# Negated scores with the sink as one more column, and the attention items of part 0 spread over all ten blocks of a group

## What is computed

```python
s = jnp.einsum('bnqkgd,bnskd->bnkgqs', q, k) * (HEAD_DIM ** -0.5)
s = s - slopes[...] * dist[...]
s = jnp.where(allowed[...], s, MASK_VALUE)
m = jnp.maximum(jnp.max(s, axis=-1), sink)
p = jnp.exp(s - m[..., None])
denom = jnp.sum(p, axis=-1) + jnp.exp(sink - m)
o = jnp.einsum('bnkgqs,bnskd->bnqkgd', p / denom[..., None], v)
y = (o * jax.nn.silu(gate)) @ w_out
```

## The kernel before

| slot | step | engine and line |
|---|---|---|
| 1 | S: scores into ps_s | PE L1003, L1004 |
| 1 | SM: scale, bias, row maximum; then neg_max, sink_arg | DVE L1351, L1358, L1359 |
| 1 | EX: four exponentials with row sum, sink_exp | ACT L1627, L1628 |
| 2 | SR: denom, recip; rows times recip | DVE L1367, L1368; GpSimd L1762 |
| 3 | TR: transposes into ps_t | PE L1022 |
| 3 | PH, PLO: high and low half, pt_hi and pt_lo | ACT L1636, DVE L1374 |
| 4 | PV: product with v into ps_o | PE L1049 |
| 4 | OG: half copy (sq<-ps_o), sum, times the gate | ACT L1645, DVE L1381, L1395 |
| 4 | YH, YL: the two halves of the result | ACT L1653, GpSimd L1741 |

## Time and profile before

### The profile page before, as it was taken

The page is one execution under the profiler, slowest core; times in us unless marked ns, Lnnn a source line. Parts: engine busy times, 40 slices in busy tenths (PEclk is TensorE's granted clock), DMA queues, the critical chain, the costliest instruction groups (busy, mean ns, idle before and its releaser), DMA issues.

```text
span 1758.8 us, 28031 instructions
## 1 busy us (share of the span) xinstructions
PE 1610.3 (92%) x9083; PEld 1373.4 (78%) x9083; DVE 869.8 (49%) x2194; ACT 746.0 (42%) x1658; POOL 417.4 (24%) x403
## 2 busy tenths in 40 slices
PE   5899699888788899999999899999998899999998
PEld 3788588878788777878887677878887687878877
DVE  3544423666663344337763345247662453257761
ACT  4333232666653422226664322246653422256552
POOL 0332143443443100112332000213232000213332
PEclk8889888999988999999999999999999999999998
DMA  8677767443443545543333555543325444543313
GB/s 299 227 268 245 247 233 248 145 145 133 156 143 105 211 168 191 196 164 128 136 120 144 180 191 189 184 151 135 120 97 191 167 174 165 192 171 121 136 59 143
DMA packets 145206, 299.86 MB, mean 170 GB/s; under 512 B 20719, under 2 KB 71231, under 8 KB 145070
## 3 DMA queue, kind: packets, MB, share of 16 engines
q1 hardware_dynamic: 145070, 298.08, 47.4%
HBM read 232.44 MB, written 65.79 MB: 170 GB/s over the span
## 4 chain that ended last, share of the span: by engine, by line
PE 71%; DVE 10%; issue 7%; ACT 7%; DMA 3%; POOL 1%; SPq 0%; DVEq 0%; ACTq 0%; POOLq 0%
PE ps_u L811 56%; PE ps_o L1049 4%; PE ps_t L1022 3%; PE ps_s L1003 2%; PE ps_s L1004 2%; ACT ps_u L1518 1%; DVE work L1351 1%; DVE ps_u L1195 1%; ACT work L1627 1%; POOL w_lo L1689 1%; DMA x_in<-in_ada_w_dram 1%; DVE work L1261 1%; DVE q_st L1235 1%; ACT silu_g L1535 1%; DVE ps_o L1381 1%
## 5 line engine op out<-in xcount | busy, mean ns | idle before, releaser
L811 PE MATMUL ps_u<-h_all_hi,w_hi 128*128 128x512 f32 (+2 forms) x1440 | 528.8, 367 | 32.2 <-DVE silu_g L1228 11.2
L811 PE MATMUL ps_u<-h_all_hi,w_lo 128*128 128x512 f32 (+2 forms) x1440 | 517.4, 359 | 0.0
L811 PE MATMUL ps_u<-h_all_lo,w_hi 128*128 128x512 f32 (+2 forms) x1440 | 517.4, 359 | 0.0
L811 PEld LDWEIGHTS ps_u<-h_all_hi,w_hi 128*128 128x128 f32 x1440 | 281.7, 196 | 82.4 <-issue 17.6
L811 PEld LDWEIGHTS ps_u<-h_all_hi,w_lo 128*128 128x128 f32 x1440 | 281.2, 195 | 36.9
L811 PEld LDWEIGHTS ps_u<-h_all_lo,w_hi 128*128 128x128 f32 x1440 | 281.6, 196 | 35.9 <-issue 1.4
L811 PE MATMUL ps_u<-y_hi,w_hi 128*128 128x512 f32 (+1 forms) x640 | 231.1, 361 | 7.1 <-POOL y_lo L1741 7.0
L811 PE MATMUL ps_u<-y_lo,w_hi 128*128 128x512 f32 (+1 forms) x640 | 228.4, 357 | 0.0
L811 PE MATMUL ps_u<-y_hi,w_lo 128*128 128x512 f32 (+1 forms) x640 | 228.3, 357 | 0.0
L1762 POOL TENSOR_TENSOR work<-work,recip 128x512 f32<-128x512 f32 (+2 forms) x136 | 132.8, 996 | 323.4 <-DVE recip L1368 323.4
L1689 POOL TENSOR_TENSOR w_lo<-w_raw,w_hi 128x1024 fp32r<-128x1024 f32 (+1 forms) x56 | 129.3, 2310 | 238.9 <-ACT w_hi L1431 207.2
(11 more groups left out here) (186 smaller groups left out, 2252.4 us busy)
## 6 DMA issues: line engine op xcount, KB each, us to landing
w_hi<-w_hi_kept SPq DMA_DIRECT2D x156, 512.0 KB, 3.5
w_lo<-w_lo_kept SPq DMA_DIRECT2D x156, 512.0 KB, 4.5
w_hi_kept<-w_hi SPq DMA_DIRECT2D x52, 512.0 KB, 5.1
w_lo_kept<-w_lo SPq DMA_DIRECT2D x52, 512.0 KB, 5.9
...
```

Source lines behind the costliest of these rows:

```text
L811: last = nc.tensor.matmul(out, w, x, start=(i == 0), stop=(i == n - 1))
```

## The change

The scale of the scores becomes negative, so row *minima* of the negated scores are taken; the scan starts from neg_sink (a value per row) instead of a constant and delivers neg_max at once. In front of the exponentials ACT writes neg_sink as one more column of each block, and the exponentials run over 257 columns with scale -1, so that their row sum is already the denominator. neg_max as an instruction of its own, sink_arg, sink_exp and denom disappear. The blocks of work are 260 columns apart.

Within a slot the order becomes S, PV, E1, SR, **SM, OG, EX**, E2, TR, PH, W, YH, PLO, YL, in all parts. In part 0, `places` puts a0 in q1-1, a1 in g0-1, a2 in g1-1, a3 in the next kv-0, a4 in q0-0 and a5 in q1-0 (the last group keeps its former places).

```diff
@@ slot @@
             out += [("PV", c)] if c is not None else []
-            out += first + to_norm + second
+            out += first + to_norm
+            out += [("SM", a)] if a is not None else []
             out += [("OG", c)] if c is not None else []
+            out += [("EX", a)] if a is not None else []
+            out += second
             out += [("TR", b), ("PH", b)] if b is not None else []
-            out += [("SM", a)] if a is not None else []
             out += [("split",)]
             out += [("YH", c)] if c is not None else []
-            out += [("EX", a)] if a is not None else []
             out += [("PLO", b)] if b is not None else []
@@ part @@
-            places = {("q1", 1): 0, ("g0", 1): 1, ("g1", 0): 2, ("g1", 1): 3, ("kv", 1): 4, ("q0", 0): 5}
+            places = {("q1", 1): 0, ("g0", 1): 1, ("g1", 1): 2, ("kv", 0): 3, ("q0", 0): 4, ("q1", 0): 5}
+            places_last = {("q1", 0): 5, ("q1", 1): 0, ("g0", 1): 1, ("g1", 0): 2, ("g1", 1): 3}
@@ SM on DVE @@
-                        last = V.tensor_tensor_reduce(out=out, in0=src, in1=b, scale=HEAD_DIM ** -0.5, scalar=LOWEST, op0=ALU.add,
-                                                      op1=ALU.max, accum_out=row_max[r, d, at:at + 1])
-                    link(last)
...
-                    link(V.scalar_tensor_tensor(out=m2(neg_max), in0=m2(row_max), scalar=-1.0, in1=ns, op0=ALU.mult, op1=ALU.min))
-                    V.tensor_tensor(m2(sink_arg), m2(neg_max), ns, ALU.subtract).then_inc(max_ready, 1)
+                        last = V.tensor_tensor_reduce(out=out, in0=src, in1=b, scale=-HEAD_DIM ** -0.5, scalar=neg_sink[r, h:h + 1],
+                                                      op0=ALU.add, op1=ALU.min, accum_out=neg_max[r, d, at:at + 1])
+                    last.then_inc(max_ready, 1)
@@ SR on DVE @@
-                    dve.wait_ge(sink_ready, a + 1)
-                    link(V.tensor_tensor(denom[r, d, 0:nb], row_sum[r, d, 0:nb], sink_exp[r, d, 0:nb], ALU.add))
-                    V.reciprocal(recip[r, d, 0:nb], denom[r, d, 0:nb]).then_inc(recip_ready, 1)
+                    dve.wait_ge(exp_ready, a + 1)
+                    V.reciprocal(recip[r, d, 0:nb], row_sum[r, d, 0:nb]).then_inc(recip_ready, 1)
@@ EX on ACT @@
+                    if a >= 2:
+                        act.wait_ge(p_turned, a - 1)
+                    put = work[r, d, 0:nb * BLOCK].rearrange("p (t e c) -> p t e c", e=2, c=BLOCK)[:, :, :, end]
+                    A(put, neg_sink[r, h0:h0 + 2].unsqueeze(1).to_broadcast([r.stop - r.start, nb // 2, 2]), ACT.Copy).then_inc(sink_put, 1)
+                    act.wait_ge(sink_put, a + 1)
...
-                        A(x, x, ACT.Exp, bias=neg_max[r, d, at:at + 1], accum_out=row_sum[r, d, at:at + 1])
-                    A(sink_exp[r, d, 0:nb], sink_arg[r, d, 0:nb], ACT.Exp).then_inc(sink_ready, 1)
+                        last = A(x, x, ACT.Exp, bias=neg_max[r, d, at:at + 1], scale=-1.0, accum_out=row_sum[r, d, at:at + 1])
+                    last.then_inc(exp_ready, 1)
```

More of the change, by code:

```diff
@@ L46 @@
 SHIFT = 2
-LOWEST = -3e38
+BLOCK = 260
 U_PROMPT = 2 * HIST
@@ L396, in part @@
                 for b, evacs in enumerate(blocks):
-                    at = places.get((what, b))
-                    a = src[at] if at is not None and src else None
+                    at = (places_last if p == 0 and g == GROUPS - 1 and what in ("q1", "g0", "g1") else places).get((what, b))
+                    from_old = p == 0 and (what, b) == ("q1", 0)
+                    its = old if from_old else src
+                    a = its[at] if at is not None and its else None
                     last = b == (1 if p == 0 else 0)
@@ L407, in part @@
                             s.append(x)
-        tail = [new[at] for (what, b), at in places.items() if what in ("kv", "q0")]
+        tail = new[4:] if p == 0 else new[3:]
         drain = [[x for x in slot(a) if x != ("split",)] for a in tail + [None, None, None]]
@@ L453, in trunk_kernel @@
         x_in = sb("x_in", [P, 2, D_MODEL])
-        work = sb("work", [P, 2, 4 * 256])
+        work = sb("work", [P, 2, 4 * BLOCK])
         pt_hi, pt_lo = sb("pt_hi", [P, 1024], F32R), sb("pt_lo", [P, 1024], F32R)
@@ L483, in trunk_kernel @@
         sinks, neg_sink = sb("sinks", [P, HEADS]), sb("neg_sink", [P, HEADS])
-        row_max, neg_max = sb("row_max", [P, 2, 4]), sb("neg_max", [P, 2, 4])
-        row_sum, sink_arg, sink_exp = sb("row_sum", [P, 2, 4]), sb("sink_arg", [P, 2, 4]), sb("sink_exp", [P, 2, 4])
-        denom, recip = sb("denom", [P, 2, 4]), sb("recip", [P, 2, 4])
+        neg_max, row_sum, recip = sb("neg_max", [P, 2, 4]), sb("row_sum", [P, 2, 4]), sb("recip", [P, 2, 4])
         flat = work[:, :, :].rearrange("p a b -> p (a b)")
@@ L1021, in _ @@
                                 o = (4 * (at // 2) + 2 * kt + e) * P
-                                last = nc.tensor.transpose(t_flat[:, o:o + P], work[:, a % 2, at * 256 + kt * P:at * 256 + (kt + 1) * P],
+                                last = nc.tensor.transpose(t_flat[:, o:o + P], work[:, a % 2, at * BLOCK + kt * P:at * BLOCK + (kt + 1) * P],
                                                            ident[:, :])
@@ L1345, in _ @@
                         if it["sample"]:
-                            out, src = work[r, d, at * 256:at * 256 + WINDOW + SAMPLE], s_flat[r, at * 256:at * 256 + WINDOW + SAMPLE]
+                            out, src = work[r, d, at * BLOCK:at * BLOCK + WINDOW + SAMPLE], s_flat[r, at * 256:at * 256 + WINDOW + SAMPLE]
                             b = bias[r, 2 * hp + e, 2 * WINDOW - WINDOW - SAMPLE:2 * WINDOW]
                         else:
-                            out, src = work[:, d, at * 256 + k0:at * 256 + 256], s_flat[:, at * 256 + k0:at * 256 + 256]
+                            out, src = work[:, d, at * BLOCK + k0:at * BLOCK + 256], s_flat[:, at * 256 + k0:at * 256 + 256]
                             b = bias[:, 2 * hp + e, k0:256]
-                        last = V.tensor_tensor_reduce(out=out, in0=src, in1=b, scale=HEAD_DIM ** -0.5, scalar=LOWEST, op0=ALU.add,
-                                                      op1=ALU.max, accum_out=row_max[r, d, at:at + 1])
-                    link(last)
-                    h0 = 4 * g + 2 * hp
-                    nt = nb // 2
-                    m2 = lambda x: x[r, d, 0:nb].rearrange("p (t e) -> p t e", e=2)
-                    ns = neg_sink[r, h0:h0 + 2].unsqueeze(1).to_broadcast([r.stop - r.start, nt, 2])
-                    link(V.scalar_tensor_tensor(out=m2(neg_max), in0=m2(row_max), scalar=-1.0, in1=ns, op0=ALU.mult, op1=ALU.min))
-                    V.tensor_tensor(m2(sink_arg), m2(neg_max), ns, ALU.subtract).then_inc(max_ready, 1)
+                        h = 4 * g + 2 * hp + e
+                        last = V.tensor_tensor_reduce(out=out, in0=src, in1=b, scale=-HEAD_DIM ** -0.5, scalar=neg_sink[r, h:h + 1],
+                                                      op0=ALU.add, op1=ALU.min, accum_out=neg_max[r, d, at:at + 1])
+                    last.then_inc(max_ready, 1)
                 elif kind == "SR":
@@ L1621, in _ @@
                     nb = 2 * len(it["tiles"])
+                    end = WINDOW + SAMPLE if it["sample"] else 256
+                    h0 = 4 * it["g"] + 2 * it["hp"]
+                    if a >= 2:
[3 more added lines that the diff above has]
+                    act.wait_ge(sink_put, a + 1)
                     act.wait_ge(max_ready, a + 1)
@@ L1625, in _ @@
                     for at, t, e, k0 in item_blocks(it):
-                        x = work[r, d, at * 256 + k0:at * 256 + (WINDOW + SAMPLE if it["sample"] else 256)]
-                        A(x, x, ACT.Exp, bias=neg_max[r, d, at:at + 1], accum_out=row_sum[r, d, at:at + 1])
-                    A(sink_exp[r, d, 0:nb], sink_arg[r, d, 0:nb], ACT.Exp).then_inc(sink_ready, 1)
+                        x = work[r, d, at * BLOCK + k0:at * BLOCK + end + 1]
+                        last = A(x, x, ACT.Exp, bias=neg_max[r, d, at:at + 1], scale=-1.0, accum_out=row_sum[r, d, at:at + 1])
+                    last.then_inc(exp_ready, 1)
                 elif kind == "PH":
@@ L1747, in _ @@
                     pool.wait_ge(recip_ready, a + 1)
-                    pool.wait_ge(sink_ready, a + 1)
+                    pool.wait_ge(exp_ready, a + 1)
                     r = slice(P - SAMPLE, P) if it["sample"] else slice(0, P)
```

12 lines of the change are left out of this document (6 added, 6 removed).

## The result

The changed kernel takes **1786.07 us** (median of 4 runs, 1784.72 to 1786.9), against 1768.99 for the kernel before in the same comparison. The ratio is 1.01, with a 95% interval of 1.0076 to 1.0123: slower by 1%, some 17 us. The prediction said 1761 with a range of 1748 to 1775. It was wrong, and on the other side of no change. The profiled execution has a span of 1785.0 us against 1758.8.

The account below looks back on a forecast made before the run. TensorE matmuls, busy 1610.3 of 1758.8 us, were taken as the bound. Part 0's -18 and parts 1 to 3's +12 gave -6: 1754.6 from the profiled 1760.57, 1761 for the median, range 1748 to 1775.

Parts of the forecast that it names:

- -18 for part 0: Part 0's attention: beginning, two full turns and end together 18 us shorter, between -8 and -23.
- +12 for parts 1 to 3: Attention of parts 1 to 3: turns, part ends and group 0 together 12 us longer, between 0 and +16.
- walk of part 0: Full turn of part 0, ten slots stepped through with measured durations: closes at 51.8 us, 53 with hand-overs, -4.2 per turn.
- Parts 1 to 3, the turn: Kv and q0 slots of each full turn in parts 1 to 3: net +1.2 us, nine times, +10.8.
- the named wait: Q0 slot in parts 1 to 3: S of a0 newly waits 1.6 us for q_lo in each full turn.
- Group 0: First group of parts 1 to 3: E2 of q1 comes 0.7 us earlier within a wait, 3 x -0.7 = -2.1.
- The end of part 0: Last stretch of part 0's attention: shorter waits for maxima, pt_lo and behind VT, -7 us, between -5.8 and -8.
- The pointer: Minimum scan starting from neg_sink instead of a constant: between 0 and 0.189 us per item, taken as 0.
- The wait behind VT: Part 0: a5's scores directly behind VT wait 2.9 us for the v copies (v_lo_ready).
- B: Slower rival: the three waits behind VT in part 0 become 6 us instead of 2.9, giving 1775; chance 0.12.
- C: Rival: turns of part 0 stay at 57 us, part 0 gives only -6, total 1773; chance 0.13.
- A: Faster rival: the new order costs nothing in parts 1 to 3, leaving -18, total 1749; chance 0.27.

Follow-up runs that it names:

- e2: Run, not the slot step E2: the kernel before with the new slot order alone, softmax and places as before: 1821.2 us, ratio 1.0331.
- e13: The changed kernel with ScalarE's former order (PH ahead of EX) in all parts: 1744.28 us, ratio 0.9898 to the kernel before.
- e1: The kernel before with the new softmax alone, slot order and places as before: 1735.13 us, ratio 0.9843.
- e7: The kernel before with the new softmax and VectorE's new order, ScalarE's order and places as before: 1749.85 us, ratio 0.9918 to the kernel before.
- e11: The kernel before with the new softmax alone, its scan starting from the constant 3e38 instead of neg_sink: 1732.79 us, ratio 0.984.

## Why the prediction was wrong, point by point

The sum was -18 for part 0 and +12 for parts 1 to 3. It came out at -5.2 and +29.0. In part 0 the beginning was given -3, the two turns -8 and the end -7; measured were -1.3, -4.3 and +0.3.

- **The step that failed: ScalarE's order.** The prediction moves EX ahead of PH in every slot. In its walk of part 0 it takes this to be free, even a help ("PH of a4 no longer stands behind a late exponential"); in parts 1 to 3 it follows the late PH, but to the wrong waits (next point). From the changed kernel to e13, which differs in that alone, it is 17.6 us in part 0 and 24.0 in parts 1 to 3, more than the whole loss. What the walk missed is that ScalarE's queue is in order too, so PH now waits for scores, transposes and scans of another item before it: PV waits 11 times, 18.1 us, against 6 times, 7.8 us, in e13. With ScalarE's order put back, the change stands at -22.8 us in part 0 and +5.0 in parts 1 to 3.
- **The walk of a turn in part 0.** A second term was too small: PE's own work. The waits that the walk names add up to 7.2 us (2.9 + 0.3 + 0.7 + 0.4 + 1.5 + 0.3 + 1.1), if all are PE's. Closing at 51.8 then leaves 44.6 for PE, and rows 2 show it busy for 48.1 to 48.4, the stretches after for 47.0. With 47.0 the walk gives 54.2 us, and 54.5 were measured. PE's waits in the first full turn after are 7.5 us in all, 2.8 behind VT as predicted, but 3.7 of PV for pt_lo, which it had gone. So the total of the waits was met by luck. Nor do the turns of e13, 50.6 and 52.2 us, bear out the 51.8: e1 has 54.1 and 52.5 without new slots, and one of the two turns of e13 ran at a lower granted clock (1.00, then 0.93, with 45.08 and 47.57 us of busy PE for 360 and 359 matmuls):

```profile
359.50:410.00 50.50, 45.08 (x360) 43.92 (x359) 33.49 (x106) 36.30 (x103) 25.59 (x25) 1.00 0.46 157
410.00:462.00 52.00, 47.57 (x359) 46.59 (x359) 33.73 (x107) 36.45 (x103) 25.58 (x25) 0.93 0.43 153
```

- **Parts 1 to 3, the turn.** The forecast was +4.0 a part, measured were +8.8 to +10.2. The chain was followed rightly as far as pt_lo (888.5 forecast, 889.5 found, of which 0.5 is that the transposes start that much later in this trace) and the copies behind it, but the prediction asked only which wait of S and PV follows. It did not ask what VT needs, which is the second of those copies: three waits of 1.3 us. Behind it S waits only 0.5 for q_lo. So the named wait came in e7 and e13, with 1.2 us, and in the changed kernel another stood in its place. No run moves the two copies ahead of pt_lo, so what VT's wait costs by itself is not shown.
- **Group 0 and the end of a part.** Group 0 was given -0.7; its step is +2.0 instead, since the VT of group 1 ends it. What follows the last VT is 4.8 us longer in part 1, where the prediction had 1.2 + 1.1; PV alone waits 2.7 us longer there (4.4 against 1.7).
- **The end of part 0.** Given -7, it is +0.3 (64.1 to 64.4). In e13 it is 56.6, which is -7.5; in e1, without new slots, it is 55.2, so this bears out the number and not its reasons.
- **The softmax.** Its share was never costed alone. e1 shows -18.6 in part 0 and -2 a part in the others, where the prediction gave the others nothing for it. The prediction saw the held 1.20 us step, and took 2 us for a sample item, near the 1.58 us that neg_max and sink_arg average there. Then it put the same gain down to the new slots.
- **The pointer.** Taken at 0 between bounds of 0 and 0.189 us per item. It is 0.24, above the upper bound, and worth some 1.3 us in each of parts 1 to 3 and 5.1 in part 0 (e1 to e11, one profile each).
- **The wait behind VT.** Given 2.9, found 2.8 all three times. Right, and so B's long wait didn't come. C's turn of 57 didn't come either (54.5). A, that parts 1 to 3 keep their time, had a chance of 0.27 and is the furthest off.
- **The sum.** The rivals all took the -18 or the +12 as a block. None had both go wrong from one cause, and so the range ended at 1775. One order is used in all parts, and a price put wrong in it is wrong in sixteen groups at once.
